# A mixture-of-experts kernel whose empty token slots are skipped by the gathers and whose drain order is changed

## Chip, cores and metric

The kernel runs on one core of one Trainium2 chip. The metric is the device time of one execution in microseconds (us); lower is better.

## What is computed

The input is 512 tokens of 1024 floats. The reference is two transformer-like blocks; this case touches the end of the first one.

```
first_block:  x = x + mixers(rms_norm(x))                       # retention and pooling
              x = x + moe(rms_norm(x))                          # 32 experts, the best 4 for each token
              x = x + sigmoid(rms_norm(x) @ ple_gate_w) * (p @ ple_proj_w)
second_block: state-space mixer, gated FFN, short convolution, gated FFN, final norm

moe:  logits = hn @ router_w + router_b; top 4, softmax gates
      for every (token, chosen expert):
          gu  = hn[token] @ w_gate_up[expert] + b_gate_up[expert]
          act = (clip(up) + 1) * (min(gate, 7) * sigmoid(1.702 * gate))
          y   = act @ w_down[expert] + b_down[expert]
      x[token] += gate * y
```

Every expert has 8 MB of up weights and 4 MB of down weights, in float32.

## The kernel before, in words

**Slots.** An expert gets a tile of CAP = 96 token slots. 512 tokens with four experts each make 2048 filled slots, and the 32 tiles have 3072, so 1024 slots are empty. The tokens of an expert are ranked from 0, so the filled slots are the first rows of its tile and the empty ones the last. Routing builds the table of token numbers by matrix products (L2440): the sum for a slot is its token's number, and 0 where no token is. L1785 casts it to integers in `smi`. An empty slot therefore names token row 0. A 33rd tile, past the last expert, is entirely empty here; the loop gathers it too, because experts with more than 96 tokens would continue there (the parts under `extra > 0` aren't run with these inputs).

**Weights.** `ring` has 12 slots of 1 MB. Slots 0 to 7 hold the up weights (one for each 128 of the 1024 input rows), slots 8 to 11 the down weights. SyncE (SP) issues every weight load: `load_up` (L595) and `load_down` (L601) wait on `s_slot_done`, which TensorE raises after the last product of a slot, and then reload that slot. All these loads stand in one queue in the order of their issue. For e = 1 to 30 the loop (L628) issues up(e+1) and down(e); down(31) comes after it (L631).

**TensorE, expert e** (L2491): four up slots (L2476), the transposes of expert e-1's hidden values (L2468), the transposes of the gathered rows of tile e+1 (L2459, `tokens_columns`), four more up slots, then the four down slots of expert e-1 (L2487). After the last expert comes down(31) (L2528), then the bias products (L2555), the transposes of `p_rows` (L2245) and its product (L2591), and then, once the outputs are combined (`got_used`), the PLE gate (L2578 to L2583).

**GpSimd (POOL)**. The first gather, of tile 0, is L800, the others are L791 in `gather`, called by `next_tile(tile)` (L795): it waits until tile `tile` has landed and has been transposed, and gathers tile `tile+1` into `xs`, 96 rows of 4 KB from `hn_dram`. `store_part(e)` (L807) waits for a piece of a table which VectorE makes once per expert (L1826) and stores it to `m_c_dram` (L809). `lag_rows` (L814) copies pieces of another table. The loop (L819 to L827) calls them in this order:

```
for e in range(4):
    next_tile(e)
    store_part(e)
```

**Drain.** After down(31)'s loads, SP loads `p_rows`, then the two halves of the PLE gate weights, `ple_w_sb[0]` and `[1]` (2 MB each, into up slots 4 and 5, and 6 and 7), the second after the first has landed (L644 to L652):

```
sp.wait_ge(s_slot_done, extra * 12 + 12 * E - 4)
...
load(p_rows, p_by_chunk, s_ple_in)
load(ple_w_sb[0], ple_gate_v[:, :, 0:512], s_ple_in)
sp.wait_ge(s_ple_in, 32)
load(ple_w_sb[1], ple_gate_v[:, :, 512:1024], s_ple_in)
```

ScalarE (ACT), after the loop: it stores y of expert 30, reads `extra` from memory into a register, makes the high parts of both PLE halves (L1131), and only then copies and stores y of expert 31 (`store_y`, L1086 and L1090). POOL waits for that store and then gathers the expert outputs of every token (L841); VectorE adds them up (L1893).

## Time and profile before

| | us |
|---|---|
| median of 3 runs | 2538.88 |
| lowest, highest | 2532.52, 2540.63 |
| the profiled execution: its time | 2532.89 |
| its span in the trace | 2531.3 |

The profiled execution took 1.6 us more than its span, for what lies around it. Expert products and weight loads take about 1060 us of the span, from 278 to 1340 us; the drain up to the first combined rows reaches to 1378 us. TensorE is busy for 97% of the span, and the DMA queues are full over the stretch of the experts. The rows are read as follows: an engine, its line, the operation, what it writes and reads, its shape, how many, and in square brackets the idle time of the engine before it and what ended it. "DMA to landing" is the time from the issue of a transfer to the semaphore that tells of its data.

### The profile page before, as it was taken

What the parts mean: (1) busy time and instruction counts of PE and PEld (TensorE: products, weight loads), DVE (VectorE), ACT (ScalarE), POOL (GpSimd) and SP (SyncE); (2) the same over time, 40 slices, a digit from 0 to 9 for tenths busy, and PEclk for the clock granted to TensorE, in tenths of its full rate; (3) what the DMA queues carried; (4) which work ended last, traced back from release to release, by engine and by line L of the source; (5) the groups of instructions that cost most, each with busy time, mean ns of one, the idle gap of its engine ahead of it and who ended that gap; (6) DMA issues with size and microseconds to landing.
All of it is one profiled execution on the core that took longest, in us unless ns stands there. A gap on an engine that the chain in (4) does not pass through costs nothing.

```text
span 2531.3 us, 47797 instructions
## 1 busy us (share of the span) xinstructions
PE 2447.0 (97%) x19810; PEld 1588.4 (63%) x19810; DVE 1134.8 (45%) x1524; ACT 558.5 (22%) x785; POOL 229.2 (9%) x385
## 2 busy tenths in 40 slices
PE   9998899999999999999996989999999999999998
PEld 7777444444443444444444787888888888888886
DVE  7878422222222222222224887688533544444332
ACT  5233200000000000000002543222322222222322
POOL 2150100000000000000003101121000000000000
PEclk9999999999999999999997999999999999999999
DMA  9535999999999999999997856577333531233432
GB/s 328 201 99 190 338 382 409 409 408 409 409 409 407 409 414 408 409 408 409 407 409 257 184 178 186 175 238 234 106 92 93 151 90 34 83 92 91 112 92 79
DMA packets 306438, 647.86 MB, mean 256 GB/s; under 512 B 29728, under 2 KB 227232, under 8 KB 256192
## 3 DMA queue, kind: packets, MB, share of 16 engines
q1 hardware_dynamic: 270528, 544.77, 59.6%
q0 software_dynamic: 19888, 82.20, 9.3%
q10 hardware_dynamic: 15952, 19.93, 2.2%
q8 instruction: 48, 0.79, 0.1%
q14 instruction: 22, 0.18, 0.0%
HBM read 620.68 MB, written 30.35 MB: 257 GB/s over the span
## 4 chain that ended last, share of the span: by engine, by line
PE 61%; issue 17%; DMA 12%; DVE 5%; SPq 2%; ACT 1%; POOL 0%; ACTq 0%; POOLq 0%; DVEq 0%
PE bank L2476 18%; DMA ring<-in_expert_w_down 9%; PE bank L2487 9%; PE bank L2756 8%; PE bank L2764 8%; PE bank L2757 8%; SPq L540 2%; PE bank L2277 1%; PE bank L2245 1%; DMA ring<-in_ple_gate_w 1%; DMA ring<-in_w_in 1%; PE bank L2468 1%; PE bank L2459 1%; PE bank L2306 1%; PE bank L2307 1%
## 5 line engine op out<-in xcount | busy, mean ns | idle before, releaser
L2476 PE MATMUL bank<-ring,work 128*32 128x512 f32 x6144 | 671.7, 593 | 2.1 <-DVE work L1798 2.1
L2476 PEld LDWEIGHTS bank<-ring,work 128*32 128x32 f32 x6144 | 196.1, 110 | 433.5 <-issue 407.1
L2487 PE MATMUL bank<-ring,ca 128*32 128x256 f32 x6144 | 341.5, 379 | 10.1 <-DMA ring<-in_expert_w_down 10.0
L2487 PEld LDWEIGHTS bank<-ring,ca 128*32 128x32 f32 x6144 | 197.3, 110 | 161.5 <-DMA ring<-in_expert_w_down 20.9
L2756 PE MATMUL bank<-h_hi,fin_hi 128*128 128x512 f32 x704 | 274.4, 390 | 1.7 <-DVE fin_lo L2065 1.7
L2757 PE MATMUL bank<-h_hi,fin_lo 128*128 128x512 f32 x704 | 273.9, 389 | 0.0
L1811 DVE COPY ca<-bank 128x768 f32<-128x768 f32 x32 | 30.7, 958 | 503.7 <-PE bank L2468 503.7
L1075 ACT ACTIVATE work<-bank 128x384 f32<-128x384 f32 x66 | 28.8, 489 | 676.5 <-PE bank L2476 675.0
L1798 DVE TENSOR_TENSOR work<-bank,nat 128x1536 f32<-128x1536 f32 x32 | 56.3, 1758 | 248.6 <-PE bank L2476 248.6
L2764 PE MATMUL bank<-h_lo,fin_hi 128*128 128x512 f32 x704 | 166.7, 389 | 0.0
L2065 DVE TENSOR_TENSOR fin_lo<-rows,fin_hi 128x1024 fp32r<-128x1024 f32 x88 | 103.7, 1222 | 126.4 <-ACT fin_hi L1281 126.0
L2756 PEld LDWEIGHTS bank<-h_hi,fin_hi 128*128 128x128 f32 x704 | 132.2, 188 | 30.8 <-issue 3.5
L2764 PEld LDWEIGHTS bank<-h_lo,fin_hi 128*128 128x128 f32 x704 | 132.2, 188 | 27.4
L2757 PEld LDWEIGHTS bank<-h_hi,fin_lo 128*128 128x128 f32 x704 | 132.2, 188 | 27.3
L2756 PE MATMUL bank<-f_hi,fout_hi 128*128 128x512 f32 x352 | 137.7, 391 | 0.0
L2757 PE MATMUL bank<-f_hi,fout_lo 128*128 128x512 f32 x352 | 137.1, 389 | 0.0
L1281 ACT ACTIVATE fin_hi<-rows 128x1024 fp32r<-128x1024 f32 x88 | 88.2, 1052 | 213.8 <-DMA rows<-in_w_ffn_in 213.8
L809 POOL DMA_DIRECT2D m_c_dram<-work x32 | 18.8, 588 | 941.6 <-DVE work L1826 941.6
L2764 PE MATMUL bank<-f_lo,fout_hi 128*128 128x512 f32 x352 | 82.4, 389 | 0.0
L1086 ACT ACTIVATE cb<-bank 128x768 f32<-128x768 f32 x32 | 25.9, 810 | 254.0 <-PE bank L2487 254.0
L1327 ACT ACTIVATE ring<-bank 128x512 f32<-128x512 f32 x60 | 35.8, 597 | 183.5 <-PE bank L2764 183.5
L858 POOL TENSOR_TENSOR sm<-sm 128x4 f32<-128x4 f32 x4 | 4.1, 1014 | 795.9 <-DVE sm L1993 795.9
(472 smaller groups left out, 3384.0 us busy)
## 6 DMA issues: line engine op xcount, KB each, us to landing
ring<-in_expert_w_gate_up SPq DMA_DIRECT2D x256, 1024.0 KB, 28.6
ring<-in_expert_w_down SPq DMA_DIRECT2D x128, 1024.0 KB, 28.5
rows<-in_w_ffn_in SPq DMA_DIRECT2D x88, 512.0 KB, 5.0
work<-in_w_ada POOLq DMA_DIRECT2D x64, 384.0 KB, 4.2
ring<-in_w_ada POOLq DMA_DIRECT2D x36, 384.0 KB, 6.3
y_dram<-cb ACTq DMA_DIRECT2D x128, 96.0 KB, 8.0
work<-in_w_ffn_out SPq DMA_DIRECT2D x8, 1408.0 KB, 7.0
rows<-in_w_ffn_out SPq DMA_DIRECT2D x8, 1408.0 KB, 7.1
```

Of the source, the lines that this page charges most:

```text
L540: sp.dma_start(dst, src).then_inc(done, 16)
L1075: act.activation(xs_t[:, 4 * r:4 * r + 4, :], ps[6 + r][:, 0:4 * CAP].rearrange("p (k t) -> p k t", k=4), ACT.Copy).then_inc(s_xst_ready, 1)
L1281: act.activation(split[n][0][b][:, v], raw[:, v], ACT.Copy).then_inc(s_w_hi, 1)
L1327: act.activation(sig_sb[b], ps[3 * b + bank][:], func).then_inc(s_lin_sig, 1)
L1798: tt(gate_up, up_ps, bias_bc.unsqueeze(1).broadcast_to([P, GROUPS, CHUNK]), ALU.add).then_inc(s_gate_up, 1)
L1811: dve.tensor_copy(dst, src).then_inc(s_hid, 1)
L2065: tt(split[n][1][at][:, v], buf[at][:, v], whole(split[n][0][b][:, v]), ALU.subtract).then_inc(s_w_lo, 1)
L2476: last = mm(ps[g][32 * c:32 * (c + 1), :], xs_t[:, k, 32 * g:32 * (g + 1)], slot[k][:, CHUNK * c:CHUNK * (c + 1)], start=(k == 0), stop=(k ...
L2487: last = mm(ps[first + g][32 * c:32 * (c + 1), 0:n], hidden[:, g, P * k + 32 * d:P * k + 32 * (d + 1)], down_slot[d][:, k, n * c:n * (c + ...
L2756: mm(ps[3 * b + v][:], w_hi[b][:, v, k, :], x_hi[:, k, :], start=(k == 0), stop=False)
L2757: mm(ps[3 * b + v][:], lo[:, v, k, :], x_hi[:, k, :], start=False, stop=False)
L2764: last = mm(ps[3 * b + v][:], w_hi[b][:, v, k, :], x_lo[:, k, :], start=False, stop=(k == depth[n] - 1))
```

## The change

- The constant `token` is now the token's number less 512, so that a filled slot sums to its number less 512 and an empty slot to 0; L1785 adds 512 when it casts. Empty slots then name row 512, one past the last row (511). L1621 compares the same constant and is adapted.
- The token gathers get a bound of 511 and skip an index beyond it without an error. `xs` is set to zero once before.
- POOL calls `next_tile(0)` first and from then on `next_tile(e + 1)` before `store_part(e)`. The third gather (tile 2), which stood behind `store_part(0)`, thus comes before it.
- SP issues the PLE halves inside the end of the expert loop: half 0 once up slot 5 of expert 31 is done, half 1 once up slot 7 is done, both ahead of the loads of down(31). `p_rows` comes after down(31) and has its own semaphore. Each half has its own semaphore, and the second no longer waits for the first. The wait for `12 * E - 4` is gone from the ordinary path.

```
-        s_ple_in = sem("ple_in")
+        s_ple_in = [sem(f"ple_in{i}") for i in range(2)]
+        s_p_in = sem("p_in")
+        s_ple_more = sem("ple_more")
...
+            def load_ple(n, done):
+                load(ple_w_sb[n], ple_gate_v[:, :, 512 * n:512 * (n + 1)], done)
+
+            for n in range(2):
+                sp.wait_ge(s_slot_done, 12 * E - 10 + 2 * n)
+                load_ple(n, s_ple_in[n])
             load_down(E - 1, E - 1, 12 * (E - 1) + 5)
+            sp.wait_ge(s_mc_stored, 16 * E)
+            load(p_rows, p_by_chunk, s_p_in)
...
-            sp.wait_ge(s_slot_done, extra * 12 + 12 * E - 4)
...
-            sp.wait_ge(s_mc_stored, 16 * E)
-            load(p_rows, p_by_chunk, s_ple_in)
-            load(ple_w_sb[0], ple_gate_v[:, :, 0:512], s_ple_in)
-            sp.wait_ge(s_ple_in, 32)
-            load(ple_w_sb[1], ple_gate_v[:, :, 512:1024], s_ple_in)
...
+            step(pool.memset(xs, 0.0))
...
-                    in_offset=bass.IndirectOffsetOnAxis(ap=smi[0:CAP, NOW_AT:NOW_AT + 1].bitcast(U32), axis=0)).then_inc(s_xs_in, 16)
+                    in_offset=bass.IndirectOffsetOnAxis(ap=smi[0:CAP, NOW_AT:NOW_AT + 1].bitcast(U32), axis=0),
+                    bounds_check=S - 1, oob_is_err=False).then_inc(s_xs_in, 16)
...
+            next_tile(0)
             for e in range(4):
-                next_tile(e)
+                next_tile(e + 1)
                 store_part(e)
...
-            with pool.Fori(1, E // 4) as block4:
+            with pool.Fori(1, E // 4 - 1) as block4:
                 for b in range(4):
-                    next_tile(4 * block4 + b)
+                    next_tile(4 * block4 + (b + 1))
                     store_part(4 * block4 + b)
                     lag_rows(block4 - 1, b)
+            for b in range(4):
+                if b < 3:
+                    next_tile(E - 3 + b)
+                store_part(E - 4 + b)
+                lag_rows(E // 4 - 2, b)
...
             def ple_weights(n):
+                act.wait_ge(s_ple_in[n], 16)
...
-            act.wait_ge(s_ple_in, 32)
             ple_weights(0)
-            act.wait_ge(s_ple_in, 48)
             ple_weights(1)
...
-            step(dve.tensor_copy(smi[:, IDS_AT:IDS_AT + TILES], ps[6][:, 0:TILES]))
+            step(ts(smi[:, IDS_AT:IDS_AT + TILES], ps[6][:, 0:TILES], float(S), None, ALU.add))
...
-            pe.wait_ge(s_ple_in, 32)
+            pe.wait_ge(s_p_in, 16)
...
-    put("token", t[:, None] + P * np.arange(NT)[None, :])
+    put("token", t[:, None] + P * np.arange(NT)[None, :] - S)
```

## Rows read from the trace of the kernel before

**Rows 1.** The page: the span.

```profile
span 2531.3 us, 47797 instructions
```

**Rows 2.** Starts of experts 2, 14 and 31 on TensorE, from the timeline.

```profile
337.17 10.48 PE L2476 MATMUL bank<-ring,work 128*32 128x512 f32 x96
...
727.94 2.33 PE L2476 MATMUL bank<-ring,work 128*32 128x512 f32 x20
...
1295.72 10.48 PE L2476 MATMUL bank<-ring,work 128*32 128x512 f32 x96
```

**Rows 3.** Windows: the experts before and after 727 us (last columns: PEclk, DMA share, GB/s).

```profile
318.00:726.00 408.00, 408.00 (x5017) 172.43 (x5013) 105.09 (x148) 33.64 (x51) 30.98 (x62) 1.00 1.02 406
728.00:1295.00 567.00, 556.92 (x6758) 230.53 (x6754) 141.87 (x204) 44.67 (x68) 43.40 (x85) 1.00 1.02 409
```

**Rows 4.** Weight loads issued in 340:350 and in 1250:1270, time to landing.

```profile
DMA to landing us min/median/max: 19.7/20.6/20.8
...
DMA to landing us min/median/max: 27.4/29.9/30.2
```

**Rows 5.** SP's timeline at the start of the expert loop.

```profile
301.08 16.93 SPq L627 DMA_DIRECT2D k_dram<-cb  x8
318.81 8.71 SPq L540 DMA_DIRECT2D ring<-in_expert_w_gate_up  x8
```

**Rows 6.** Loads of down(30), issued 1288.0 to 1296.1 us, time to landing.

```profile
DMA to landing us min/median/max: 28.6/29.0/29.4
```

**Rows 7.** The drain on TensorE, ACT, POOL and VectorE, from the timeline.

```profile
1307.60 10.51 PE L2476 MATMUL bank<-ring,work 128*32 128x512 f32 x96
...
1326.62 13.16 PE L2487 MATMUL bank<-ring,ca 128*32 128x256 f32 x240
...
1330.32 2.73 ACTq L1090 DMA_DIRECT2D y_dram<-cb  x4
...
1344.34 3.78 PE L2555 MATMUL bank<-work 32*128 32x512 f32 x8 [4.57 <-issue]
...
1352.41 5.01 ACT L1131 ACTIVATE ple_w_hi<-ring,vec 128x512 fp32r<-128x512 f32 x8 [3.19 <-DMA ring<-in_ple_gate_w]
...
1357.32 0.79 ACT L1086 ACTIVATE cb<-bank 128x768 f32<-128x768 f32 x1
...
1364.62 9.93 PE L2591 MATMUL bank<-work,ca 128*128 128x512 f32 x16 [0.78 <-ACT ca L925]
...
1377.98 1.97 PE L2245 MATMUL bank<-const,rows 128*128 128x128 f32 x8 [3.43 <-DVE rows L1893]
```

**Rows 8.** Timeline around the first three gathers.

```profile
256.07 1.29 POOL L780 COPY cb<-work 128x512 f32<-128x512 f32 x2
...
264.57 2.50 DVE L1745 TENSOR_TENSOR work<-const,work 128x512 f32<-128x512 f32 x4
...
270.27 0.21 DVE L1785 CAST smi<-bank 128x54 int32<-128x54 f32 x1 [1.66 <-PE bank L2440]
...
270.82 1.01 POOL L800 DMA_INDIRECT work<-hn_dram,smi  x1 [13.46 <-DVEq L1786]
...
315.67 0.88 PE L2459 MATMUL bank<-const,work 96*128 96x96 f32 x8 [1.61 <-DMA work<-hn_dram,smi]
```

**Rows 9.** Window 1400:1420 (as rows 3), and the page's row of its loads.

```profile
1400.00:1420.00 20.00, 20.00 (x90) 15.38 (x89) 18.09 (x20) 9.44 (x17) 6.36 (x10) 1.00 1.13 152
...
ring<-m_t_dram SPq DMA_DIRECT2D x8, 512.0 KB, 26.0
```

**Rows 10.** Windows of the drain (last columns: PEclk, DMA share, GB/s).

```profile
1345.00:1355.00 10.00, 3.12 (x8) 0.73 (x4) 7.19 (x11) 6.81 (x12) 0.00 (x0) 0.50 0.84 315
...
1343.00:1370.00 27.00, 14.84 (x31) 6.29 (x32) 15.39 (x20) 12.25 (x21) 5.97 (x7) 0.50 0.57 194
...
1377.00:1384.00 7.00, 5.34 (x16) 4.26 (x17) 4.93 (x6) 2.34 (x4) 2.48 (x3) 0.51 0.73 293
```

**Rows 11.** Line L791, 32 token gathers from 278.1 to 1279.8 us.

```profile
DMA to landing us min/median/max: 6.5/8.8/10.5
```

More of the change, by code:

```diff
@@ L634, in _ @@
             with sp.If(extra > 0):
+                for landed in s_ple_in:
+                    sp.wait_ge(landed, 16)
                 with sp.Fori(0, extra) as n:
@@ L641, in _ @@
                     load_down(n + E, expert, n * 12 + 12 * E - 3)
-            sp.wait_ge(s_slot_done, extra * 12 + 12 * E - 4)
+                sp.wait_ge(s_slot_done, extra * 12 + 12 * E - 4)
+                for n in range(2):
+                    load_ple(n, s_ple_more)
             sp.wait_ge(s_norm_in, 112)
@@ L801, in _ @@
                 out=xs, out_offset=None, in_=hn_dram,
-                in_offset=bass.IndirectOffsetOnAxis(ap=smi[0:CAP, IDS_AT:IDS_AT + 1].bitcast(U32), axis=0)).then_inc(s_xs_in, 16)
+                in_offset=bass.IndirectOffsetOnAxis(ap=smi[0:CAP, IDS_AT:IDS_AT + 1].bitcast(U32), axis=0),
+                bounds_check=S - 1, oob_is_err=False).then_inc(s_xs_in, 16)
             pool.wait_ge(s_bias_in, 32)
@@ L1127, in _ @@
                     sigmoid(n + E)
+                act.wait_ge(s_ple_more, 32)
             def ple_weights(n):
+                act.wait_ge(s_ple_in[n], 16)
                 for k in range(KD):
@@ L1620, in bbar_slabs @@
                 sign = sm[:, 192:193]
-                step(ts(sign, token[:, 0:1], NS - 0.5, 2.0, ALU.is_gt, ALU.mult))
+                step(ts(sign, token[:, 0:1], NS - 0.5 - S, 2.0, ALU.is_gt, ALU.mult))
                 step(ts(sign, sign, -1.0, None, ALU.add))
```

## Prediction

> **What bounds the kernel now.** The page gives the span, 2531.3 us [rows 1]. All edits lie between 256 and 1378 us, so I read how fast the experts go round. Expert 2 starts on TensorE at 337.17, expert 14 at 727.94, expert 31 at 1295.72 [rows 2]. That is 390.77 / 12 = 32.56 us for an expert in the first stretch and 567.78 / 17 = 33.40 in the second. The windows say what differs: up to 726 us TensorE is busy all the time, afterwards 556.9 of 567 us. The DMA share is 1.02 in both, at 406 and 409 GB/s [rows 3]. So the DMA engines are full from the start. TensorE needs 32.56 us, the transfers 33.40, and TensorE first lives on loaded slots. A load issued around 345 us lands after 20.6 us, one around 1260 us after 29.9 [rows 4]: the queue grew until it had eaten the lead. From expert 14 on, 17 x 0.84 = 14.2 us are lost. **The end of the loop is set by the DMA chain**, from 318.8 us, when SP is through with its table stores and issues weights again [rows 5], to the landing of down(30)'s last load, 1296.1 + 29.4 = 1325.5 [rows 6].
>
> The drain is a chain of waits. Down(30) and down(31) end on TensorE at 1339.8. ACT finishes the second PLE half at 1352.41 + 5.01 = 1357.4, and only then copies y of expert 31. The last product thus waits 17.5 us for work that doesn't need it [rows 7]. The combined rows of the first 128 tokens reach TensorE at 1377.98.
>
> **The start of the loop: 0.** The cast of the 54 table columns becomes an addition of the same size, nothing. Zeroing `xs` is a POOL operation of 96x1024; its nearest row copies 2 x 128x512 in 1.29 us and ends at 257.4, and VectorE needs what POOL signals next only at 264.57 [rows 8]. 7.2 us of cover; past that it would cost one for one. The first gather (issue at 270.82, taking 1.01 us) stands ahead of the first product and of SP's loads, so its own change counts in full. No row shows a gather with a bound. Bounds: a third fewer rows (32 x 4 KB = 0.13 MB) at 409 GB/s, -0.3 us; issue time doubled, +1.0. I take 0. The other gathers have 20 us and more of slack.
>
> **The third gather: 0.** TensorE waits 1.61 us for it once [rows 8]. The gather then goes out some 18 us earlier, behind the transposes of tile 1, and the wait goes. But the DMA chain starts at 318.8, when SP is through, and is full from there. TensorE gains a lead and loses it later. Bounds 0 and -1.6; 0 holds while transfers set the end. In the loop each gather now leaves before the store of the table piece, about 5 us earlier; the store waits 1.5 us more on POOL (two small copies and the issue), and VectorE wants its buffer again an expert later. 0.
>
> **The empty slots: -1.0.** Bytes first: of the gathers after 318.8 us, tiles 3 to 31 leave out about 928 rows and tile 32 all 96, together 1024 x 4 KB = 4.19 MB, which is 10.3 us at 409 GB/s. It would all count, as it is less than the 14.2 us lost. The other bound is 0. Which one depends on whether every part of the DMA path gets lighter. The skipped rows are always the last of a tile, partitions 64 to 95 on average, and a weight slot is ready only when its slowest part has landed. Does it matter where a transfer goes in SBUF? The window 1400:1420 holds mainly eight loads of 512 KB to 16 partitions each. There the DMA share is 1.13 at 152 GB/s, while 128 partitions get 409 at 1.02 [rows 3, 9]. A transfer is therefore bound by the partitions that it reaches, and partitions 0 to 63 get as many rows as before. I take the low end: nothing from tiles 3 to 31, and all of the empty tile 32, 0.39 MB or 0.96 us.
>
> The Trainium skill gives a rule that speaks against this edit (SBUF — State Buffer, "Door 1: The DMA port swizzle"): partitions 0 to 63 share eight of the sixteen ports, and 64 to 127 the other eight, so leaving out rows 64 to 95 lightens only ports that weren't the fullest. By it this term is -1.0, by bytes alone -10.3. Rows 9 agree with the first.
>
> **The drain: -3.5.** Up slots 5 and 7 of expert 31 are done at 1307.6 + 5.3 = 1312.9 and 1318.1 [rows 7]. There the PLE halves now go into the queue, ahead of down(31). Those loads stand behind them, on SP's queue and on the DMA engines. The price: 4.19 MB; with such transfers 315 GB/s were moved at a share of 0.84 [rows 10], so 375 when full, 11.2 us.
> - Down(30) has landed at 1325.5. Then 11.2 us for PLE, 1.0 for y of expert 30, and 2.6 for each MB: down(31) lands from 1340.3 to 1348.0. TensorE, through with down(30) at about 1329.4, now idles 11 us. That is the new wait.
> - The clock. After the idle time from 1339.8 the granted clock was 0.50, 1.2 GHz, from 1343 to 1370; after the one before 1377.98 it was 0.51 up to 1384, 6 us into the work [rows 10]. The first quarter of down(31) takes 5.3 us instead of 2.63. The rest run at 2.4 GHz: TensorE ends at 1340.3 + 5.3 + 7.9 = 1353.5. At full clock throughout: 1348.0 + 2.7 = 1350.7; at half throughout: 1340.3 + 21.1 = 1361.4.
> - ACT is free at 1333.1 from y of expert 30, reads its register (TensorE idled 4.57 us at the same place) and makes both halves in 10 us, up to 1347.7: hidden behind down(31), unless this ended before 1347.7.
> - So y of expert 31 is copied at 1353.5, not 1357.3: -3.8. POOL's gathers and VectorE's sums follow at the same distance.
> - What is late next: TensorE reads its register (4.6 us) after down(31), and L2555 (now 2 x 3.78 us in one piece), the transposes and L2591 (up to 9.93) end around 1374.5, when the combined rows now come, 1374.2. +0.3 at the half and full clock mixed as before, up to +3.5 all at half.
>
> Together -3.5, between -6.6 and +4.2.
>
> **Sum.** 0 + 0 - 1.0 - 3.5 = -4.5 us. The profiled execution took 2532.9, so 2528.4; it lies 6 us under the median of the runs, 2538.9, from which I get **2534.4 us**. A measurement of this kernel can tell about 0.3%, 7.6 us, from no change.
>
> **The rivals.**
> 1. *Bytes count, not places.* Then skipping gives -10.3 and the whole -13.8: 2525.1. For it: the share of 1.02 speaks of the engines as full, and if an engine's rows are spread over the tile each is relieved. Against it: rows 9. Chance 0.22. The Trainium skill (DMA: Bandwidth & Descriptors, "Why a DMA increments its semaphore by 16 and not by 1") has direct copies cut into consecutive shares, which would leave the engines of the first rows as full as before; no run here shows it for a gather.
> 2. *The PLE loads ahead of down(31) cost more than they hide (slower).* Place: TensorE's idle time from 1329.4 to 1340.3. Price: if the clock stays at 1.2 GHz through down(31), y of expert 31 is copied at 1361.4, +4.1; with tile 32's -1.0 this is +3.1, 2542.0. It decides once down(31) ends after 1357.3. If the products behind it are also late (+3.5) and the first gather dearer (+1.0), 2546.5. For it: 27 us at 0.50 in rows 10 with TensorE busy for 15 of them. Against: the 6 us. Chance 0.12.
> 3. *The drain gives all it can*, clock full: -6.6 - 1.0 = -7.6, 2531.3. Against: the idle time of 11 us. Chance 0.12.
> 4. *Skipped rows are fetched or replaced all the same*: -3.5, 2535.4. No row tells. Chance 0.06.
>
> My forecast has 0.48.
>
> **Numbers.** The range takes in rival 1 with the better drain (-10.3 - 6.6 = -16.9, 2522.0) and rival 2 with part of its extras: 2522 to 2544. Faster by over 0.3%: rival 1 (0.22), half of rival 3 (0.06), the fast edge of my forecast, where some tiles with few tokens do relieve the path (0.08): 0.36. Slower: most of rival 2, 0.10. Within 0.3%: 0.54.
>
> **What would show it.** Experts up to about 14 still take 32.56 us. After them 33.4 if I am right on the empty slots; about 33.0, with the waits starting some experts later, if rival 1 is. A gather lands in 8.8 us now [rows 11]: the same for me, clearly less for rival 1. Tile 2's wait of 1.61 us is gone. In the drain TensorE waits about 11 us for a load of down(31), under a clock of 0.50, and ends at 1353 less what the loop gained; ACT copies y of expert 31 right behind it. I am wrong if down(31) isn't late at all, or if the loop's end moves by over 3 us.

## The result, and the profile after

| | before | after | ratio of the runs | 95% interval |
|---|---|---|---|---|
| first measurement, median of 6 | 2539.43 us | 2518.61 us | 0.9930 | 0.9911 to 0.9950 |
| again, beside the experiments | 2535.67 us | 2523.43 us | 0.9956 | 0.9940 to 0.9971 |
| the profiled execution, its time | 2532.89 us | 2520.95 us | | |

The change makes the kernel faster by 0.4 to 0.7%, 11 to 18 us; I had forecast 4.5 us. One of the first six executions of the changed kernel took 5075.6 us; the ratio leaves it out.

The two profiled executions are 12.0 us apart in span. The timeline of TensorE says where [rows 2], and two windows show the stretches before and after its first waits in the loop [rows 3] (columns as there).

```profile
span 2519.3 us, 47795 instructions
```

```profile
278.02 10.51 PE L2495 MATMUL bank<-ring,work 128*32 128x512 f32 x96
...
334.83 1.04 PE L2495 MATMUL bank<-ring,work 128*32 128x512 f32 x8
...
660.48 1.04 PE L2495 MATMUL bank<-ring,work 128*32 128x512 f32 x8
...
1290.02 10.48 PE L2495 MATMUL bank<-ring,work 128*32 128x512 f32 x96
```

```profile
318.00:660.00 342.00, 342.00 (x4228) 145.23 (x4224) 88.39 (x124) 28.33 (x43) 24.57 (x48) 1.00 1.01 406
660.00:1290.00 630.00, 623.17 (x7576) 288.69 (x7570) 158.62 (x228) 50.34 (x76) 49.00 (x95) 1.00 1.01 410
```

These are the starts of experts 0, 2, 12 and 31 (before: 278.50, 337.17, 662.81, 1295.72). Up to expert 12 each takes 32.56 us, as before. From there (1290.02 - 660.48) / 19 = 33.13, where it was 33.40. But the waits begin two experts earlier. SP's timeline shows a later start of the chain: its eight table stores took 20.66 us to issue, not 16.93, and the first weight load behind them went out at 322.07, not 318.81 [rows 5]. The transfers then stay full to the end, and loads take 23.8 us to land at the start and 27.9 at the end [rows 4: 20.6 and 29.9]; down(30)'s last load is issued at 1290.4 and lands at 1318.7 [rows 6: 1325.5].

```profile
300.60 20.66 SPq L629 DMA_DIRECT2D k_dram<-cb  x8
322.07 5.02 SPq L542 DMA_DIRECT2D ring<-in_expert_w_gate_up  x8
```

```profile
DMA to landing us min/median/max: 22.0/23.8/23.9
...
DMA to landing us min/median/max: 27.1/27.9/28.4
...
DMA to landing us min/median/max: 26.8/27.7/28.3
```

A skipped row isn't free of a packet. The page of before and that of after count the same packets; 1120 of them (1024 empty slots, and the 33rd tile's 96) moved under the 512 B line, and 4.58 MB are gone. In the trace's records these are packets of 4 bytes that take 10 ns; one of 4096 bytes takes some 188. The gathers (L802) still land in 8.6 us [rows 11: 8.8].

```profile
DMA packets 306438, 647.86 MB, mean 256 GB/s; under 512 B 29728, under 2 KB 227232, under 8 KB 256192
```

```profile
DMA packets 306438, 643.28 MB, mean 255 GB/s; under 512 B 30848, under 2 KB 228352, under 8 KB 256192
...
DMA to landing us min/median/max: 5.0/8.6/9.2
```

The drain [rows 7], on TensorE, ACT, SP, POOL and VectorE, and its windows [rows 10]:

```profile
1333.36 13.25 PE L2506 MATMUL bank<-ring,ca 128*32 128x256 f32 x192 [9.65 <-DMA ring<-in_expert_w_down]
1349.78 7.20 PE L2574 MATMUL bank<-work 32*128 32x512 f32 x16 [3.17 <-issue]
1359.66 8.63 PE L2610 MATMUL bank<-work,ca 128*128 128x512 f32 x16 [0.78 <-ACT ca L944]
1369.48 1.09 PE L2264 MATMUL bank<-const,rows 128*128 128x128 f32 x8 [1.20 <-DVE rows L1912]
...
1328.52 9.92 ACT L1152 ACTIVATE ple_w_hi<-ring,vec 128x512 fp32r<-128x512 f32 x16 [3.93 <-issue]
1346.77 0.81 ACT L1105 ACTIVATE cb<-bank 128x768 f32<-128x768 f32 x1 [8.33 <-PE bank L2506]
...
1307.32 7.63 SPq L542 DMA_DIRECT2D ring<-in_ple_gate_w  x2
...
1353.99 1.06 POOL L860 DMA_INDIRECT ring<-y_dram,smi  x1 [0.72 <-issue]
...
1364.18 5.25 DVE L1912 SCALAR_TENSOR_TENSOR rows<-ring,sm,rows 128x1024 f32<-128x1024 f32 x4 [5.94 <-DMA ring<-y_dram,smi]
```

```profile
1328.00:1339.00 11.00, 5.64 (x56) 3.11 (x60) 9.72 (x15) 9.92 (x16) 0.00 (x0) 0.53 0.98 401
...
1363.00:1377.00 14.00, 12.06 (x45) 7.35 (x43) 11.23 (x10) 2.24 (x4) 8.73 (x8) 1.00 0.75 303
```

TensorE waits 9.65 us for down(31), which now stands behind the PLE halves; the granted clock is 0.53 in the window around its start (1.2 GHz for nearly all of it), and the work ends at 1346.6. ACT has both PLE halves ready at 1338.4 and copies y of expert 31 right behind down(31). From 1349 to 1363 the granted clock is 0.51 once more, and from 1363 it is 1.00, through the first work on the combined rows.

**Where the 12.0 us are.** I cut the span at four events: the start of expert 0, the start of expert 31, the combined rows of the first 128 tokens on TensorE (1377.98 and 1369.48), and the first issue of `m_t` to the later loads (1397.84 and 1386.95).

| | before | after | |
|---|---|---|---|
| start to expert 0 | 278.50 | 278.02 | -0.5 |
| expert 0 to expert 31 | 1017.22 | 1012.00 | -5.2 |
| expert 31 to combined rows | 82.26 | 79.46 | -2.8 |
| combined rows to `m_t` | 19.86 | 17.47 | -2.4 |
| `m_t` to the end | 1133.4 | 1132.4 | -1.0 |

### The profile page after: what moved, and what is told of

It is laid out like the page before. It is cut to its first block, busy times and chain, and to the rows that moved or that the text cites. A ratio compares the mean times of both kernels' runs of the same rounds, so it can differ in the third digit from the quotient of the medians.

```text
span 2519.3 us, 47795 instructions
## 1 busy us (share of the span) xinstructions
PE 2445.5 (97%) x19810; PEld 1616.7 (64%) x19810; DVE 1134.8 (45%) x1524; ACT 558.7 (22%) x785; POOL 231.2 (9%) x386
## 2 busy tenths in 40 slices
DMA packets 306438, 643.28 MB, mean 255 GB/s; under 512 B 30848, under 2 KB 228352, under 8 KB 256192
## 4 chain that ended last, share of the span: by engine, by line
PE 59%; issue 16%; DMA 14%; DVE 7%; SPq 2%; ACT 1%; POOL 0%; ACTq 0%; POOLq 0%; DVEq 0%
PE bank L2495 18%; DMA ring<-in_expert_w_down 12%; PE bank L2506 9%; PE bank L2775 8%; PE bank L2783 8%; PE bank L2776 8%; SPq L542 2%; DMA ring<-in_w_in 1%; PE bank L2296 1%; PE bank L2487 1%; PE bank L2264 1%; PE bank L2478 1%; PE bank L2325 1%; PE bank L2327 1%; PE bank L2326 1%
## 5 line engine op out<-in xcount | busy, mean ns | idle before, releaser
L2495 PEld LDWEIGHTS bank<-ring,work 128*32 128x32 f32 x6144 | 206.7, 110 | 422.8 <-issue 398.7
L2506 PEld LDWEIGHTS bank<-ring,ca 128*32 128x32 f32 x6144 | 218.0, 110 | 150.0 <-issue 43.0
L798 POOL COPY smi<-smi 128x1 int32 (+1 forms) x32 | 6.3, 196 | 850.4 <-PE bank L2478 850.4
```

The source lines that it names most:

```text
L2495: last = mm(ps[g][32 * c:32 * (c + 1), :], xs_t[:, k, 32 * g:32 * (g + 1)], slot[k][:, CHUNK * c:CHUNK * (c + 1)], start=(k == 0), stop=(k ...
L2506: last = mm(ps[first + g][32 * c:32 * (c + 1), 0:n], hidden[:, g, P * k + 32 * d:P * k + 32 * (d + 1)], down_slot[d][:, k, n * c:n * (c + ...
```

## The experiments

A caution first. Expert 0 started anywhere from 274.6 to 285.6 us in the 20 traces, in no relation that I can see to the edits, nearly all of which lie behind it. This stretch alone spreads the times by 11 us. The windows show the clock at work in it: two traces in the same 20 us, at 1.00 and expert 0 at 278.5 (before), and at 0.66 and expert 0 at 285.6 (m7 below).

```profile
240.00:260.00 20.00, 18.17 (x201) 16.39 (x203) 16.56 (x44) 11.22 (x20) 4.87 (x8) 1.00 0.85 338
```

```profile
240.00:260.00 20.00, 18.63 (x99) 17.25 (x97) 13.49 (x30) 6.23 (x11) 2.66 (x5) 0.66 0.68 263
```

So beside the times I use three lengths of each trace: **loop**, from expert 0 to expert 31; **drain**, from expert 31 to the first issue of `m_t`; and the **pace** of the transfers, the time from one landing of a slot's load to the next (the slope of a straight line through the landings of experts 3 to 30, mean of the slots).

### One part at a time

Each is the kernel before with one part of the change: the lines of the diff above on the constant, the bound and the zeroing; those on POOL's order; those on the drain.

> The kernel before with the skipped empty slots alone; gather order and drain as before. Theory A (the transfers of the experts form one full chain and the chain gets shorter by the bytes, wherever they lie in the tile): the chain starts at 318.8 as before and is 4.19 MB / 0.409 = 10 us shorter, so down(30)'s last load lands near 1315.5, expert 31 starts near 1286, time -10 us against the kernel before. Rival B (skipped rows relieve only part of the path; what the changed kernel showed, 5.7 us earlier at expert 31, is all that they can give): expert 31 starts near 1290, time -6. Rival C (my prediction's low end, places count): expert 31 starts near 1295, time -1.

> The kernel before with the new order of the token gathers alone, all 96 rows fetched, drain as before. Theory A: TensorE's wait of 1.6 us before expert 2 goes, but the gather of tile 2 now runs among the loads of expert 1, SP gets through its table stores some 3 us later (first load of up(2) issued at 322 instead of 318.8), and as the chain sets the end, expert 31 starts 2 to 3.5 us later: 1298 to 1299, time +2 to +3. Rival B (the later start of the chain has another cause, such as the zeroing or the skipping gather): first load of up(2) issued near 318.8, expert 31 at 1295.7 or up to 0.5 before, time 0.

> The kernel before with the PLE halves ahead of down(31) alone. Theory A: the loop is as before (expert 31 at 1295.7), TensorE waits some 10 us for down(31), y of expert 31 is copied 3.8 us earlier than before (1353.5), and the work behind it finds the clock at 1.0 instead of 0.50, which gives some 3 us more: time -4 to -7. Rival B (the warm clock came from something else than the drain's order): -3.5 to -4 with the clock at 0.50 around 1370 to 1380. Rival C (nothing but the loop's end counts): 0.

| | time / before | interval | loop | drain | pace |
|---|---|---|---|---|---|
| before | 1 | | 1017.2 | 102.1 | 33.42 |
| e1, empty slots | 0.9976 | 0.9962 to 0.9991 | 1010.9 | 102.9 | 33.25 |
| e2, order of gathers | 0.9996 | 0.9979 to 1.0013 | 1016.5 | 103.6 | 33.39 |
| e3, drain | 0.9976 | 0.9959 to 0.9993 | 1013.3 | 95.0 | 33.31 |
| m0 (below), order and drain | 0.9970 | 0.9958 to 0.9981 | 1015.2 | 97.0 | 33.28 |
| after | 0.9930 | 0.9911 to 0.9950 | 1012.0 | 96.9 | 33.19 |
| a0, after again | 0.9956 | 0.9940 to 0.9971 | 1011.8 | 96.2 | 33.20 |

The empty slots give 6 us of time (2 to 10 by the interval), the order nothing that can be seen (within 5), the drain 6 (2 to 10). With the drain's old order (three traces) its length is 102.1 to 103.6, with the new one (four) 95.0 to 97.0: a mean of 6.6 less. Without skipping (four) the loop takes 1013.3 to 1017.2, with it (three) 1010.9 to 1012.0: 4.0 less. Together 10.6, which fits the second measurement (11). A single trace is a weak witness: e3's loop is 3.9 us shorter than that of before, and nothing in its loop was changed. The skipping's bytes would be 10 us (Theory A of e1); that is more than e1's time and loop gave.

In e2 the first load of up(2) goes out 42.2 us after expert 0, before 40.3, after 44.1. The later start comes with the order: it is 39.6 to 40.3 us in the three traces with the old order, and 39.6 to 44.2, on average 42.2, in the fifteen with the new one and the table stores unmoved. In the time it is too small to be seen; Theory A's 2 to 3.5 us at expert 31 aren't there.

The wait of 1.61 us for the third gather is gone in e2, but expert 2 comes only 0.2 us sooner behind expert 0 (58.5 us, before 58.7). TensorE has a wait of 2.1 us for VectorE in front of the first up slots of expert 1, in every trace. In six of them (e1, e2, m2, m4, m8, d0) the granted clock then falls to 0.5 for a stretch, and the 96 products take 12.20 us instead of 10.51; in the other fourteen it stays at 1.00 there. No run shows what decides between the two. The first line is e2's, the second its window:

```profile
306.17 12.20 PE L2482 MATMUL bank<-ring,work 128*32 128x512 f32 x96 [2.08 <-DVE work L1804]
```

```profile
306.00:312.00 6.00, 5.83 (x40) 1.74 (x44) 4.01 (x6) 1.30 (x2) 0.60 (x1) 0.72 1.02 419
```

In e3 the drain alone is changed. From the combined rows to `m_t` it takes 17.5 us, like the other three of this table with the drain's new order; before, e1 and e2 take 19.9 to 21.0. The eight transposes of the combined rows take 1.09 us in e3 and 1.97 in e2. Rival B of e3 (the higher clock has another cause) falls. The lines are e3's and e2's:

```profile
1365.42 1.09 PE L2255 MATMUL bank<-const,rows 128*128 128x128 f32 x8 [0.20 <-DVE rows L1903]
```

```profile
1381.01 1.97 PE L2251 MATMUL bank<-const,rows 128*128 128x128 f32 x8 [3.90 <-DVE rows L1899]
```

> The changed kernel once more, beside the next three, with more runs than its first measurement (0.993 of the kernel before). If the single parts add up (skipping 0.9976, order 0.9996, drain 0.9976), 0.995; if the parts help one another, 0.993.

Taken singly they multiply to 0.995, and the two measurements of the whole are 0.9930 and 0.9956: the parts add up as far as this can tell.

### How the skipped rows count

The next kernels fetch given rows, whatever they hold: m1 to m7 leave out the expert inputs of some tokens. TensorE does the same work in all. The table's constant is again the token's number; a column added in the cast pushes chosen rows over the bound:

```
-            step(ts(smi[:, IDS_AT:IDS_AT + TILES], ps[6][:, 0:TILES], float(S), None, ALU.add))
+            step(ts(smi[:, IDS_AT:IDS_AT + TILES], ps[6][:, 0:TILES], skip_rows, None, ALU.add))
...
+    put("skip", S * (t[:, None] >= 64))        # m1; 0 in m0, t % 3 == 2 in m2, t < 32 in m3, t // 6 % 3 == 2 in m4
```

> The changed kernel (bound, zeroing, gather order and drain as in it), but empty slots name row 0 again, so that all 96 rows of a tile are fetched. The yardstick for the next three. All theories: the weight loads land 33.3 to 33.4 us per expert apart (the kernels without skipping so far: 33.42, 33.39, 33.31; those with it 33.19, 33.25); the time as with order and drain alone, some 6 us under the kernel before.

> As the yardstick, but rows 64 to 95 of every tile are skipped whatever they hold (this leaves a third of the tokens' expert inputs out; 1056 rows against the changed kernel's 1120). Theory A (each of the 16 DMA engines has six neighbouring rows of a gather, so only the last five or six engines are relieved, and loads wait for the fullest engine for part of their time): 0.10 to 0.2 us less per expert than the yardstick, time -3 to -6 against it. Rival B (bytes count wherever they lie): 0.32 less per expert, -9 to -10. Rival C (places count, my prediction): 0.

> As the one before, with the same number of skipped rows, but every third row of a tile (2, 5, 8 and so on), so that each engine has two rows fewer. Theory A: the full 0.32 us per expert by bytes, -9 to -10 us against the yardstick, 4 to 6 us better than with rows 64 to 95. Rival B: the same as with rows 64 to 95. Rival C (partition halves, my prediction): two thirds of the skipped rows lie in partitions 0 to 63, where half of the ports are full, so some 0.2 per expert, -6.

> As the two before, but rows 0 to 31 skipped. Theory A: as with rows 64 to 95, other engines are relieved, 0.10 to 0.2 less per expert. Rival B: 0.32 less. Rival C (partitions 0 to 63 are the full half, and all skipped rows lie there): 0.32 less, 9 to 10 us better than rows 64 to 95.

> As with every third row skipped, but in whole groups of six: rows 12 to 17, 30 to 35, 48 to 53, 66 to 71, 84 to 89 of every tile, 30 rows in five groups spread over the tile (their tokens are left out). Theory A (six neighbouring rows are one DMA engine's share): five engines are wholly relieved and eleven not at all, so 0 to 0.25 us less per expert than with no row skipped (33.28), as with the last 32 (0.07) and the first 32 (0.25), 2522 to 2527 us. Rival D (the gain comes from skipped rows being spread over the partitions, shares play no part): 0.5 less per expert, 2510 to 2513 us.

| | skipped | time / before | interval | loop | pace | engines ahead |
|---|---|---|---|---|---|---|
| m0 | none | 0.9970 | 0.9958 to 0.9981 | 1015.2 | 33.28 | 0 |
| m1 | last 32 | 0.9957 | 0.9939 to 0.9974 | 1012.7 | 33.21 | 4.7 |
| m3 | first 32 | 0.9950 | 0.9933 to 0.9967 | 1006.9 | 33.03 | 4.6 |
| m4 | 5 groups of 6 | 0.9961 | 0.9945 to 0.9977 | 1009.6 | 33.22 | 4.4 |
| m2 | every third | 0.9900 | 0.9881 to 0.9918 | 1002.9 | 32.71 | 0 |

The last column is the plainest evidence. A gather raises its semaphore 16 times, once for each DMA engine, and the trace keeps the times. I counted the engines that were through over 1 us ahead of the last (mean of 27 gathers). Before, all 16 are through within about 0.6 us. With the last 32 rows skipped, 4.7 are ahead; 32 rows are five and a third shares of six. With five whole groups of six it is 4.4, with every third row none. So **six neighbouring rows are one engine's share**. The Trainium skill (DMA: Bandwidth & Descriptors, "Why a DMA increments its semaphore by 16 and not by 1") says of some direct copies that each of the 16 engines gets a sixteenth of the partitions, rounded up, which would be six of 96; these gathers agree, and show that the six are neighbours. The count needs full engines: in m6 (below), where they idle at times, 4.6 are ahead although the shares are even.

Rival D of m4 (being spread over the partitions is enough) falls: m4's rows are spread, and its time and pace are those of m1, 15 us above m2's (2525.2 and 2510.1). So does Rival B: of 32 skipped rows, where each costs the same bytes, m1 gains 3.5 us of time and m2 19.3 (medians 2529.4, 2525.9, 2510.1). That is twice what Theory A gave m2: 12.3 us come in the loop and 10.0 in the drain. In m2 TensorE no longer waits over 0.1 us for anything from expert 3 on; its loop is the 1001.2 us of TensorE's own work (m6, s0) and the 1.7 us at half clock told of above. A weight slot is ready when its slowest sixteenth has landed. In the changed kernel the empty slots are the last of a tile; its gathers show 5.3 engines ahead. In this window of the DMA view (800 to 1200 us) the gather's relief is there in m1 as in m2 (q0 from 5.8% down), but the up loads land as late as ever in m1. Last column: median us to landing.

```profile
q0 software_dynamic: 2496, 7.87, 5.8%
...
ring<-in_expert_w_gate_up SPq DMA_DIRECT2D x96, 1024.0 KB, 29.1
```

```profile
q0 software_dynamic: 2496, 6.30, 4.7%
...
ring<-in_expert_w_gate_up SPq DMA_DIRECT2D x97, 1024.0 KB, 28.7
```

```profile
q0 software_dynamic: 2496, 6.30, 4.5%
...
ring<-in_expert_w_gate_up SPq DMA_DIRECT2D x99, 1024.0 KB, 19.8
```

These are m0, m1 and m2.

### Shares or places

m2 gained 0.57 us per expert, more than its bytes (0.13 MB at 409 GB/s, 0.32 us). So I cut the gather anew: 64 rows instead of 96, which makes shares of four, into the same partitions (m5, m7), into 32 to 95 (m6); and all 96 into 32 to 127 (m8).

```
-                    out=xs, out_offset=None, in_=hn_dram,
-                    in_offset=bass.IndirectOffsetOnAxis(ap=smi[0:CAP, NOW_AT:NOW_AT + 1].bitcast(U32), axis=0),
+                    out=xs[0:64], out_offset=None, in_=hn_dram,
+                    in_offset=bass.IndirectOffsetOnAxis(ap=smi[0:64, NOW_AT:NOW_AT + 1].bitcast(U32), axis=0),
```

> As with rows 64 to 95 skipped, the same places and the same bytes, but the gather itself names only rows 0 to 63 (rows 64 to 95 are left out). Theory A: 64 rows are cut into 16 shares of four, every engine is relieved, 0.5 us less per expert than with no row skipped, 15 to 20 us less time than with rows 64 to 95 skipped by the bound: 2508 to 2513. Rival C (places): the time with rows 64 to 95 skipped, 2526. Rival E (a skipped row's packet of 4 bytes still costs much): between, as the 32 packets are gone too.

> The gather of 64 rows to partitions 0 to 63 once more, beside the one above: 32.95 to 33.05 us per expert, 1004 to 1005 us from the loop's start to expert 31.

> As the gather of 64 rows, but they are written to partitions 32 to 95 instead of 0 to 63 (the tiles hold the tokens of ranks 0 to 63 in those rows, rows 0 to 31 stay zero). The gather of 64 rows gave 0.28 us per expert, the number by bytes, spread rows 0.5 to 0.57. Rival C in part (partitions play a part once all engines are relieved: rows within 0 to 63 keep one half of the path full): some 0.2 us less per expert than with rows to 0 to 63 (33.00), 32.8 or less, and the end of the loop 3 us earlier (1004.6 us after its start there, 1001.2 where TensorE sets the pace). Theory A alone (only the engines' shares matter; what is left comes from the skipped rows' place between fetched ones): 33.0 and 1004.6 again.

> The kernel with no row skipped (33.28 us per expert, 1015.2 us from the loop's start to expert 31, 0.997 of the kernel before), but the gathers write their 96 rows to partitions 32 to 127 instead of 0 to 95; TensorE still transposes partitions 0 to 95, so that part of the tokens' inputs is left out, and no byte of a transfer. Theory F (a fetched row costs the weight loads by the half of the partitions that it goes to, and 0 to 63 are the full half: 64 of the 96 rows go there in the kernel, 32 here): 0.5 to 1 us less per expert, 1001 to 1003 us to expert 31, time -15 to -20 against 2529, although every byte is still moved. Rival (partitions count only once bytes are saved): 33.2 to 33.3 and 1013 to 1015 us.

| | rows to 0-63 / 64-127 | shares | time / before | interval | loop | pace |
|---|---|---|---|---|---|---|
| m0 | 64 / 32 | even, 6 | 0.9970 | 0.9958 to 0.9981 | 1015.2 | 33.28 |
| m8 | 32 / 64 | even, 6 | 0.9977 | 0.9961 to 0.9993 | 1016.1 | 33.35 |
| m1 | 64 / 0 | uneven | 0.9957 | 0.9939 to 0.9974 | 1012.7 | 33.21 |
| m5 | 64 / 0 | even, 4 | 0.9923 | 0.9895 to 0.9951 | 1004.6 | 33.00 |
| m7 | 64 / 0 | even, 4 | 0.9929 | 0.9911 to 0.9947 | 1003.3 | 32.95 |
| m3 | 32 / 32 | uneven | 0.9950 | 0.9933 to 0.9967 | 1006.9 | 33.03 |
| m2 | 43 / 21 | even, 4 of 6 | 0.9900 | 0.9881 to 0.9918 | 1002.9 | 32.71 |
| m6 | 32 / 32 | even, 4 | 0.9911 | 0.9892 to 0.9930 | 1001.2 | 32.22 |

Pairs with nearly one difference: m1 and m5 have the same rows in the same partitions and differ in shares, 0.21 to 0.26 us per expert and 8 to 9 us of loop. (m5 also lacks the 32 packets of 4 bytes. They are at most six in an engine's share, 0.06 us, so Rival E falls.) Against m0, m5 gains 0.28, about half of Theory A's 0.5; m2, with 43 rows in the fuller half instead of 64, gains the rest. m3 and m6 have the same partitions and differ in shares, 0.81. m1 and m3 both have uneven shares and differ in partitions, 0.18 and 6 us of loop (Rival C of m3 wanted 0.32 less per expert and 9 to 10 us of time; the times are 2 us apart); m7 and m6 both have even shares, 0.73. So **both count**, and most together. The DMA view of m7 and m6, same window:

```profile
q0 software_dynamic: 2112, 6.29, 4.8%
...
ring<-in_expert_w_gate_up SPq DMA_DIRECT2D x99, 1024.0 KB, 26.9
```

```profile
q0 software_dynamic: 2112, 6.29, 4.0%
...
ring<-in_expert_w_gate_up SPq DMA_DIRECT2D x100, 1024.0 KB, 7.1
```

The same bytes of the gathers took a sixth less of the engines' time (4.0% and 4.8% of the window), and the loads land 7.1 us after their issue: the chain no longer sets the end, TensorE does (1001.2 is the shortest loop that any kernel here had). As the engines now idle at times, 32.22 is no measure of what they can do, only a bound. The single packets say the same: of 4096 bytes they took 195 ns on average in m7 and 163 in m6; of 8192 bytes, the weights', 318.2 and 315.9.

m8 told me that I had the reason wrong. Theory F, that partitions 0 to 63 are the full half in themselves, wanted 0.5 to 1 us less; it got nothing. The reading that I take is that the fuller of the two halves counts: 64 rows in m0 (0 to 63), 64 in m8 (64 to 127), 32 in m6. This is what the Trainium skill has (SBUF — State Buffer, "Door 1: The DMA port swizzle"): partitions 0 to 63 reach eight of the sixteen ports, 64 to 127 the other eight. m0, m8 and m6 agree with it. It isn't shown alone, though. m8 also fits its own rival, that partitions count only once bytes are saved; a gather of 96 rows, 48 to each half, would decide and wasn't run. And m6 changes with the halves which engine writes to which partitions. Open stays too how the two effects act together: by the packets' times, (318.2 - 315.9) ns x 96 packets of weights and 32 ns x 4 of the gather, 0.35 us of the 0.73 per expert are accounted for.

### Versions that use it

s0 gives each share of six its part of the empty slots; nothing is left out. Routing places rank r in row 6 x (r mod 16) + r / 16, and ACT undoes it as it copies the transposed columns:

```
-                of_row = [P, TOPK, P]
-                tt(row_hot[:, n, :], iota.unsqueeze(1).broadcast_to(of_row),
-                   pick_r[:, n].unsqueeze(2).broadcast_to(of_row), ALU.is_equal).then_inc(s_slot_hot, 1)
+                of_row = [P, TOPK, 6, 16]
+                tt(row_hot[:, n, 0:CAP].rearrange("p n (b a) -> p n a b", a=6),
+                   iota[:, 0:CAP].rearrange("p (a b) -> p a b", a=6).unsqueeze(1).broadcast_to(of_row),
+                   pick_r[:, n].unsqueeze(2).unsqueeze(3).broadcast_to(of_row), ALU.is_equal).then_inc(s_slot_hot, 1)
...
-                    act.activation(xs_t[:, 4 * r:4 * r + 4, :], ps[6 + r][:, 0:4 * CAP].rearrange("p (k t) -> p k t", k=4),
+                    act.activation(xs_t[:, 4 * r:4 * r + 4, :].rearrange("p k (a b) -> p k a b", a=6),
+                                   ps[6 + r][:, 0:4 * CAP].rearrange("p (k b a) -> p k a b", k=4, a=6),
```

t0 is the changed kernel with the table stores among the weight loads; s2 has both:

```
             sp.wait_ge(s_k_sb, 5)
             for v in range(CH):
+                sp.wait_ge(s_slot_done, 9 + v)
+                load_slot(v, 2)
                 sp.dma_start(k_dram[:, :, 2 * CH - 2 - v, :], k_sb[GC * v:GC * (v + 1), :, :]).then_inc(s_k_out, 16)
-            with sp.Fori(1, E - 1) as e:
+            load_down(1, 1, 17)
+            with sp.Fori(2, E - 1) as e:
```

d0 has down(31)'s loads ahead of the PLE halves again, and in ACT `store_y` of expert 31 ahead of `ple_weights`.

> The changed kernel with the empty slots spread over the tile: the token of rank r goes to row 6 x (r mod 16) + r / 16, so each group of six neighbouring rows holds its share of the empty ones, and ACT reads the transposed columns back into rank order; the outputs are the same. Theory A (a group of six rows is one DMA engine's, and the fullest engine sets the pace): as with every third row skipped, 0.5 us less per expert than with no row skipped, weight loads that keep landing near 20 us, the end of the loop set by TensorE's 32.56 us; some 10 us under the changed kernel. Rival (the gain with every third row came from those rows' partitions, or from leaving tokens out): the time of the changed kernel, +-2.

> The changed kernel with SP's eight table stores issued one by one, each behind a load of up(2), instead of in one row ahead of them. Theory A (between 301 and 322 SP issues no weights, and the DMA engines moved 94 to 236 GB/s from 310 to 325): the first load of up(2) goes out right after up(1)'s last, at 305 instead of 322; the chain gains 3 to 6 us, expert 31 starts as much earlier: time -3 to -5. Rival B (the small packets of the stores cost the engines the same wherever they are issued): 0 to -1.

> The changed kernel with the PLE halves behind down(31) again, each as soon as its slots are free, and ACT copying and storing y of expert 31 ahead of the PLE halves. Theory A (of what the kernel before lost in the drain, 17.5 us, the place of y's copy was all, and the new order only exchanged it for a wait of TensorE): TensorE doesn't wait for down(31), y of expert 31 is copied 12 us earlier than in the changed kernel (56.8 us after the start of expert 31 there, 45 here), and the first combined rows come 8 to 12 us earlier: time -8 to -12. Rival B (the gathers of y now run into the PLE loads, 12 MB in all, 30 us, and the PLE weights are late for the gate): half or less of it stays, -0 to -5.

> The version with spread empty slots, beside the next one: 2505 to 2509 us.

> Spread empty slots and SP's table stores among the loads of up(2). Theory A (the weight loads still fall behind TensorE by 0.15 us per expert, which shows only at down(31), late by some 4 us): the chain starts earlier, and of that 2 to 4 us arrive at down(31) and behind it: -2 to -4 against the version with spread slots. Rival (TensorE now sets the pace, so an earlier start of the chain is worth nothing): 0.

| | time / before | interval | loop | drain | pace |
|---|---|---|---|---|---|
| a0, after | 0.9956 | 0.9940 to 0.9971 | 1011.8 | 96.2 | 33.20 |
| t0 | 0.9942 | 0.9927 to 0.9957 | 1008.3 | 96.5 | 33.18 |
| d0 | 0.9953 | 0.9936 to 0.9970 | 1011.2 | 95.9 | 33.23 |
| s0 | 0.9878 | 0.9860 to 0.9896 | 1001.2 | 89.4 | 32.71 |
| s1, s0 again | 0.9918 | 0.9888 to 0.9947 | 1001.2 | 89.6 | 32.77 |
| s2 | 0.9884 | 0.9853 to 0.9915 | 1001.2 | 88.0 | 32.79 |

**Spreading the empty slots gives more than the whole change did**: 18 us under it on the same chip (2505.3 and 2523.4), where 10 were expected. The repeat s1 gives less, 0.9918 of the kernel before or some 10 us under the changed kernel, but its lengths are those of s0, 17 us shorter together. The loop is TensorE's, 10.6 us shorter, and the drain 6.8, as down(31) lands with less of a backlog ahead of it: TensorE waits 3.45 us for it, not 9.65. In s2 it is 2.66. It is Theory A's end of the loop; the loads land in 22.2 us. The timeline of s0, and of s2:

```profile
1283.85 10.48 PE L2497 MATMUL bank<-ring,work 128*32 128x512 f32 x96
...
1320.99 13.27 PE L2508 MATMUL bank<-ring,ca 128*32 128x256 f32 x192 [3.45 <-DMA ring<-in_expert_w_down]
```

```profile
1315.72 12.25 PE L2511 MATMUL bank<-ring,ca 128*32 128x256 f32 x192 [2.66 <-DMA ring<-in_expert_w_down]
```

t0 did shorten the loop by 3.5 us, as expected (the 94 to 236 GB/s of its expectation are the kernel before's, from 310 to 320 us; the changed kernel moved 127 to 227 there); the windows 310:325 of after and of t0 show the gap closed, 161 to 363 GB/s:

```profile
310.00:325.00 15.00, 15.00 (x150) 5.52 (x146) 3.74 (x9) 0.28 (x1) 1.97 (x4) 1.00 0.76 161
```

```profile
310.00:325.00 15.00, 15.00 (x142) 5.35 (x138) 4.13 (x10) 0.00 (x0) 2.57 (x5) 1.00 1.05 363
```

Its time (2522.5 beside 2523.4) doesn't show it clearly, and on top of spread slots it gains 1.6 us of drain; the 8.5 us between s1 and s2 (2513.0, 2504.5) are more than their lengths explain, expert 0 having started 5 us apart.

d0 failed to gain, with its y copied 44.6 us after the start of expert 31 where the changed kernel takes 56.8. On its timeline ACT first waits for the store of expert 30's y (0.5 us past the end of down(31)), and POOL for that of expert 31's: both stores stand behind the 4 MB of the PLE halves, and land in 5.7 to 8.0 us. In the changed kernel those of expert 31 took 1.8 to 3.7.

```profile
1341.16 0.81 ACT L1105 ACTIVATE cb<-bank 128x768 f32<-128x768 f32 x1 [9.99 <-DMA y_dram<-cb]
...
1345.82 10.69 DVE L1900 SCALAR_TENSOR_TENSOR ple_w_lo<-ring,vec,ple_w_hi 128x512 fp32r<-128x512 f32 x16 [17.26 <-ACT ple_w_hi L1152]
...
1352.11 4.46 POOL L869 TENSOR_TENSOR smi<-smi 128x1 int32<-128x1 int32 x1 [34.95 <-DMA y_dram<-cb]
...
1372.25 1.97 PE L2264 MATMUL bank<-const,rows 128*128 128x128 f32 x8 [2.24 <-DVE rows L1912]
```

Counted from expert 31, y is copied 12.2 us sooner than in the changed kernel. The stores take 4.7 us of that. Nearly 4 more go in one small operation of POOL (L869), which takes 4.46 us where it takes 0.19 in the changed kernel; it ends at 1356.6, as VectorE's row of sixteen (L1900) ends at 1356.5. In the changed kernel that row is over at 1340, long before. What holds POOL no run isolates. The combined rows thus come 3.8 us sooner, and behind them TensorE is at 1.2 GHz again: the transposes take 1.97 us, and up to `m_t` it takes 20.2 us, not 17.5. One us or less is left.

So PLE ahead of down(31) has merits that I hadn't seen: its bytes, and the work on them, are out of the way when y is stored, and the clock is high behind the combined rows.

## Why the prediction was wrong

**The start of the loop, 0.** Right: expert 0 started 0.5 us earlier, the first gather landed in 4.5 us (before 4.6).

**The third gather, 0.** Right in size, as far as the time tells: 0.9996. TensorE's wait went (in the changed kernel expert 2 starts 56.8 us after expert 0, before 58.7), and the lead was lost later. I had put the chain's start at 318.8 unmoved; it moved by 3.8 us relative to expert 0 in the profiled pair and by 2.3 on average. That the moved gather, among expert 1's loads, is what delays the table stores is likely and not shown.

**The empty slots, -1.0.** This term failed. The loop got 4.0 us shorter on average over the traces, e1's time 6. The step was "a transfer is bound by the partitions that it reaches, and partitions 0 to 63 get as many rows as before". Rows 9 do show that places matter, and m3 and m6 bear it out, m6 far beyond what I gave it. But I made it the only limit. The other limit is the engine: m1 and m5 differ by 8 to 9 us of loop with the very same rows. Rival 1, by bytes (-10.3), was as wrong on the other side, and its own text has the reason: the consecutive shares, which leave the engines of the first rows as full as before. That they hold for a gather, m4 and the landings show. The real tiles are uneven, some with fewer than 64 tokens, and let 4.0 us of loop through where m1 gave 2.5; the difference is within what single traces spread.

**The drain, -3.5.** This term was mis-sized: it measured -6.6 on average. It had two stretches. Up to the combined rows, where my sum ends, the forecast was -3.5 and the traces have -3.7 (expert 31 to combined rows 82.5 us with the old order, 78.8 with the new). The mechanism was right there: TensorE waits 9.65 us for down(31) (11 forecast), starts on it at half clock, and the copy of y follows right behind. That the number came out is partly luck, of two misses. Y of expert 31 was copied 5.0 us sooner, not 3.8. In the changed kernel down(31) was there 43.3 us after the start of expert 31, not 44.6, and took 13.2 as forecast; in e3 and m0, with nothing skipped, it was there at 44.8 as forecast, but less of it ran at half clock and it took 12.1. And what was late next cost 1.4 us, not 0.3: in the changed kernel the stores of y landed in up to 3.7 us.

Behind the combined rows I counted nothing, and gave no reason: "follow at the same distance" took the work there to run as before. That is the step of the drain that failed. It ran at 1.00 where it had run at 0.51 [rows 10], the eight transposes in 1.09 us instead of 1.97, and from there to `m_t` it took 17.5 us instead of 20.4, 2.9 less. TensorE had been busy from 1349.8 with waits of 0.8 and 1.2 us only, the clock at 0.51 at first and at 1.00 from 1363 on; before, it had waited 3.43 us [rows 7], and in d0, where the clock was low again, 2.24.

**The sum.** -4.5 forecast; by the lengths -10.6, of the times -11 to -18. The drain was short by 3.1 us, the empty slots by 3.0. The result lies below my range in the first measurement, and just inside it in the second (2523.4, low end 2522). The spread of the start (11 us between traces) had no place in my range either, which was drawn around one median of 3 runs.

## What to carry to other kernels

When rows are left out of a transfer, ask of each DMA engine and of each half of the partitions what it has left, not of the bytes: leave out the same number in each engine's share of neighbouring rows, and then spread what stays over partitions 0 to 63 and 64 to 127 (shown here for 64 rows, not for 96). And compare traces stage by stage from a common event; a stretch that no edit touches can spread the times by more than the edit is worth.

## What was not expected of the hardware

- A row skipped by the bound is still a packet, of 4 bytes and 10 ns; the number of packets didn't change (306438), nor did the cut into shares (m1 against m5).
- A gather's 96 rows are cut into 16 shares of six neighbours. A gather of 64 rows has even shares too, which makes four (m5 and m7: no engine over 1 us ahead).
- 64 rows into partitions 32 to 95 instead of 0 to 63 took the landing of the weight loads from 26.9 to 7.1 us: 163 ns for a packet of 4 KB, not 195.
- Small stores that were issued beside 4 MB of loads on another queue landed in 5.7 to 8.0 us instead of 1.8 to 3.7.
- A POOL operation on 128x1 took 4.46 us instead of 0.19 and ended as a long row of VectorE did (d0).
- Behind the same wait of 2.1 us TensorE's clock fell to half in six traces, which cost 1.7 us, and stayed full in fourteen.
